# Attention rows divided by their sums inside the transposing product, with a scaled identity as its moving operand

## The reference

```python
sc = einsum(q, k) * scale          # with a causal, banded or bias mask
p = softmax(sc, axis=-1)
o = einsum(p, v)
# differential: pd = p[:, 0] - lam * p[:, 1], then o = einsum(pd, v)
```

## Time and profile before

| | |
|---|---|
| median of 3 runs | 2713.63 us (2712.52 to 2717.51) |
| profiled execution | 2710.46 us |
| its span, first to last instruction | 2709.1 us |
| mean granted TensorE clock | 0.932 of full |
| busy: PE, PEld, DVE, ACT, POOL | 90%, 67%, 66%, 45%, 17% |

### The profile page before, as it was taken

One profiled execution on the slowest core, in us unless ns is written; L12 is line 12 of the kernel. 1 busy time (PEld: TensorE's weight loads), 2 busy tenths in 40 slices (PEclk: granted clock), 3 DMA queues, 4 the chain that ended last, 5 costly groups with the idle time before them and its releaser, 6 DMA issues.

```text
span 2709.1 us, 27512 instructions
## 1 busy us (share of the span) xinstructions
PE 2437.1 (90%) x10999; PEld 1808.0 (67%) x10999; DVE 1797.2 (66%) x2013; ACT 1220.8 (45%) x1435; POOL 455.4 (17%) x467
## 2 busy tenths in 40 slices
PE   3986899897899889999897786999999999999997
PEld 2444698544498737454796645878787878787785
DVE  4666476476298534454565415888888888888886
ACT  1132453213254301222442115767676777777774
POOL 1045371034265100053232000000000000000000
PEclk9977999895799979999898897999999999999998
DMA  7631377461247705303365423999999999898994
GB/s 278 252 148 47 128 276 275 163 267 43 94 159 279 271 26 221 141 4 128 132 269 218 176 100 123 337 355 340 348 341 353 341 347 348 336 354 335 359 346 180
DMA packets 49504, 625.78 MB, mean 231 GB/s; under 512 B 8551, under 2 KB 9240, under 8 KB 11672
## 3 DMA queue, kind: packets, MB, share of 16 engines
q1 hardware_dynamic: 43632, 618.42, 60.4%
q10 hardware_dynamic: 4072, 5.40, 0.7%
q0 software_dynamic: 1664, 0.11, 0.0%
HBM read 622.85 MB, written 1.05 MB: 230 GB/s over the span
## 4 chain that ended last, share of the span: by engine, by line
PE 78%; DVE 10%; ACT 4%; issue 3%; DMA 2%; POOL 2%; ACTq 0%; DVEq 0%; SPq 0%; POOLq 0%
PE psum L1068 17%; PE psum L1069 17%; PE psum L1070 17%; PE psum L957 5%; PE psum L984 4%; DVE sbuf L684 4%; PE psum L2106 3%; PE psum L1101 2%; PE psum L1146 2%; PE psum L2100 2%; DVE ring_r L1063 1%; PE psum L2014 1%; DMA ring<-in_t_ffn 1%; PE psum L829 1%; PE psum L2588 1%
## 5 line engine op out<-in xcount | busy, mean ns | idle before, releaser
L1063 DVE TENSOR_TENSOR ring_r<-ring,sbuf_r 128x2048 fp32r<-128x2048 f32 (+1 forms) x309 | 566.6, 1837 | 183.0 <-ACT sbuf_r L1054 182.0
L1069 PE MATMUL psum<-ring_r,sc_r 128*128 128x512 f32 x1688 | 667.6, 396 | 0.0
L1054 ACT CAST sbuf_r<-ring 128x2048 fp32r<-128x2048 f32 (+1 forms) x309 | 468.6, 1518 | 359.9 <-PE psum L1070 307.9
L1063 DVE TENSOR_TENSOR ring_r<-ring,sc_r 128x2048 fp32r<-128x2048 f32 (+1 forms) x221 | 451.5, 2048 | 148.9 <-ACT sc_r L1054 147.2
L1054 ACT CAST sc_r<-ring 128x2048 fp32r<-128x2048 f32 (+1 forms) x221 | 374.3, 1700 | 264.8 <-PE psum L1070 163.5
L1068 PE MATMUL psum<-sbuf_r,sc_r 128*128 128x512 f32 (+1 forms) x1236 | 466.4, 377 | 14.7 <-DVE sc L2430 14.0
L1070 PE MATMUL psum<-sbuf_r,sc_r 128*128 128x512 f32 x948 | 375.5, 396 | 0.0
L1069 PEld LDWEIGHTS psum<-ring_r,sc_r 128*128 128x128 f32 x1688 | 318.8, 189 | 73.9 <-issue 3.1
L684 DVE SCALAR_TENSOR_TENSOR sbuf<-ring,sbuf 128x512 f32<-128x512 f32 x416 | 341.6, 824 | 21.8 <-DMA ring<-in_t_ada 16.2
L1068 PE MATMUL psum<-sc_r 128*128 128x512 f32 x740 | 299.3, 405 | 1.0 <-DVE sc_r L2620 1.0
L1070 PE MATMUL psum<-sc_r 128*128 128x512 f32 x740 | 291.1, 393 | 0.0
(11 more groups left out here) (293 smaller groups left out, 2901.4 us busy)
## 6 DMA issues: line engine op xcount, KB each, us to landing
ring<-in_t_moe SPq DMA_DIRECT2D x168, 2048.0 KB, 7.8
ring<-in_t_ada SPq DMA_DIRECT2D x48, 2048.0 KB, 8.3
ring<-in_t_mlp SPq DMA_DIRECT2D x32, 2048.0 KB, 8.5
ring<-in_t_win SPq DMA_DIRECT2D x17, 2048.0 KB, 8.3
ring<-in_t_ffn SPq DMA_DIRECT2D x16, 2048.0 KB, 8.4
ring<-in_t_out SPq DMA_DIRECT2D x7, 2048.0 KB, 8.3
ring<-in_t_bias SPq DMA_DIRECT2D x2, 2048.0 KB, 10.4
ring<-in_t_win SPq DMA_DIRECT2D x1, 1664.0 KB, 8.8
```

The source lines that it names most:

```text
L1054: p.act.e.copy(p.r(hi), src).then_inc(*p.sig("high", st.tag, n))
L1063: p.dve.e.tensor_tensor(p.r(src), src, p.r(hi), ALU.subtract).then_inc(*p.sig("lowp", st.tag, n))
L1069: e.matmul(out, l[0], r[1], start=False, stop=False)
```

## The change

Exponentials are no longer divided by their sums before they are transposed. POOL makes a diagonal matrix of 128x128 from the identity and the reciprocals of the job, and for a "second" job times the negated lambda as well. PE multiplies: the block of exponentials is the stationary operand, the diagonal the moving one, and the product is the transposed block with each query's column divided by its sum. It is an FP32 matmul in place of a transpose. For a differential pair both jobs are multiplied into the same PSUM block, the first with `start`, the second with `stop`; the mix on DVE and its small multiply are gone. The reciprocal is moved to the end of DVE's round, behind the evacuations of older jobs. Each stage has three or four buffers for diagonals (`DG`), and a diagonal waits until the product that read its buffer last is done.

```diff
@@ def pe_turned(p, A, i):
-    p.pe.wait_ge(*scaled_at(p, A, i))
+    p.pe.wait_ge(*p.at("diag", A.tag, i))
...
+    jobs = (i - 1, i) if j.kind == "second" else (i,)
     for m, c in enumerate(j.blocks):
-        ins = p.pe.e.transpose(tp[:, 128 * m:128 * m + 128], A.P[i % len(A.P)][:, c:c + 128], p.IDENT)
+        for q in jobs:
+            ins = p.pe.e.matmul(tp[:, 128 * m:128 * m + 128], A.P[q % len(A.P)][:, c:c + 128], A.DG[q % len(A.DG)],
+                                start=(q == jobs[0]), stop=(q == i))
     ins.then_inc(*p.sig("turned", A.tag, j.nth))
@@ def dve_softmax(p, A, i):   (now dve_max and dve_over)
     e.tensor_reduce(nd, sp[:, 0:j.cols], X_AXIS, ALU.max, negate=True).then_inc(*p.sig("max", A.tag, i))
+def dve_over(p, A, i):
     p.dve.wait_ge(*p.at("exp", A.tag, i))
     e.reciprocal(sm, sm).then_inc(*p.sig("over", A.tag, i))
-    if j.kind == "second":
-        pa = A.P[i % 4][:, 0:j.cols]
-        p.dve.wait_ge(*p.at("over", A.tag, i))
-        p.dve.link(e.tensor_tensor(sm, sm, p.LAM[:, 2:3], ALU.mult))
-        p.dve.wait_ge(*p.at("scaled", A.tag, i - 1))
-        e.scalar_tensor_tensor(out=pa, in0=pa, scalar=sm, in1=A.P[(i - 1) % 4][:, 0:j.cols], op0=ALU.mult,
-                               op1=ALU.add).then_inc(*p.sig("mixed", A.tag, i))
@@ def act_exp(p, A, i):
-        if A.jobs[k].kind == "first":
-            p.act.wait_ge(*p.at("mixed", A.tag, k + 1))
-        else:
-            p.act.wait_ge(*p.at("turned", A.tag, A.jobs[k].nth))
+        p.act.wait_ge(*used_at(p, A, k))
@@ def pool_scale(p, A, i):   (now pool_diag)
-    pa = A.P[i % len(A.P)][:, 0:j.cols]
     p.pool.wait_ge(*p.at("over", A.tag, i))
-    p.pool.e.tensor_scalar(pa, pa, p.SUMS[:, i % 8:i % 8 + 1], None, ALU.mult).then_inc(*p.sig("scaled", A.tag, i))
+    if i >= len(A.DG):
+        p.pool.wait_ge(*used_at(p, A, i - len(A.DG)))
+    sm, out = p.SUMS[:, i % 8:i % 8 + 1], A.DG[i % len(A.DG)]
+    if A.jobs[i].kind == "second":
+        ins = p.pool.e.tensor_scalar(out, p.IDENT, sm, p.LAM[:, 2:3], ALU.mult, ALU.mult)
+    else:
+        ins = p.pool.e.tensor_scalar(out, p.IDENT, sm, None, ALU.mult)
+    ins.then_inc(*p.sig("diag", A.tag, i))
@@ def dve_round(p, A, one, two, end):
     if one is not None:
-        dve_softmax(p, A, one)
+        dve_max(p, A, one)
     if two is not None:
         put_turned(p, p.dve, "D", A, two)
     if end is not None:
         put_values(p, p.dve, "D", A, end)
+    if one is not None:
+        dve_over(p, A, one)
```

More of the change, by code:

```diff
@@ L447, in stages @@
         self.dil = dil = Heads("dil", [U[:, i, 1440:2208] for i in range(2)], [xn[:, 0:1536], sc[:, 18432:19968]],
-                               [(0, 1), (2, 3)], [(4, 5)], 1)
+                               [(0, 1), (2, 3)], [(4, 5)], 1, [sc[:, 19968 + 128 * i:20096 + 128 * i] for i in range(3)])
         every = self.MASKB.rearrange("p (g s n) -> p g s n", g=3, s=2)[:, :, 1, :]
@@ L468, in stages @@
         self.mla = mla = Heads("mla", [sc[:, 16896 + 256 * i:17152 + 256 * i] for i in range(4)],
-                               [xn[:, 512 * i:512 * i + 512] for i in range(2)], [(i,) for i in range(4)], [(4,), (5,)], 2)
+                               [xn[:, 512 * i:512 * i + 512] for i in range(2)], [(i,) for i in range(4)], [(4,), (5,)], 2,
+                               dil.DG)
         for h in range(8):
@@ L491, in stages @@
                                [sc[:, 13312 + 512 * i:13824 + 512 * i] for i in range(2)],
-                               [(i,) for i in range(4)], [(4,), (5,)], 3)
+                               [(i,) for i in range(4)], [(4,), (5,)], 3,
+                               [sc[:, 16640 + 128 * i:16768 + 128 * i] for i in range(4)])
         for h in range(4):
@@ L539, in stages @@
         self.na = na = Heads("na", [sc[:, 6168 + 512 * i:6680 + 512 * i] for i in range(4)], [XN[:, i, :] for i in range(2)],
-                             [(i,) for i in range(3)], [(3,), (4,)], 2)
+                             [(i,) for i in range(3)], [(3,), (4,)], 2, [sc[:, 14400 + 128 * i:14528 + 128 * i] for i in range(4)])
         for h in range(16):
@@ L612, with __init__ @@
 class Heads:
-    def __init__(self, tag, P, PT, s_banks, t_banks, depth):
+    def __init__(self, tag, P, PT, s_banks, t_banks, depth, DG):
         self.tag, self.P, self.PT, self.s_banks, self.t_banks, self.depth = tag, P, PT, s_banks, t_banks, depth
+        self.DG = DG
         self.jobs, self.heads, self.groups, self.turned = [], [], 0, []
@@ L1102, in pe_scores, with used_at @@
     ins.then_inc(*p.sig("score", A.tag, i))
-def scaled_at(p, A, i):
-    return p.at("mixed" if A.jobs[i].kind == "second" else "scaled", A.tag, i)
+def used_at(p, A, i):
+    return p.at("turned", A.tag, A.jobs[i + 1 if A.jobs[i].kind == "first" else i].nth)
 def pe_turned(p, A, i):
@@ L1152, in group_bank, with dve_max @@
     return next(h.bank for h in A.heads if h.group == g)
-def dve_softmax(p, A, i):
+def dve_max(p, A, i):
     e = p.dve.e
@@ L1159, in dve_softmax @@
     sp = A.span(p, A.s_banks[i % len(A.s_banks)])
-    nd, sm = p.ND[:, i % 8:i % 8 + 1], p.SUMS[:, i % 8:i % 8 + 1]
     p.dve.wait_ge(*p.at("score", A.tag, i))
@@ L1168, in dve_softmax @@
         p.dve.wait_ge(*p.at("biased", i))
-    e.tensor_reduce(nd, sp[:, 0:j.cols], X_AXIS, ALU.max, negate=True).then_inc(*p.sig("max", A.tag, i))
+    e.tensor_reduce(p.ND[:, i % 8:i % 8 + 1], sp[:, 0:j.cols], X_AXIS, ALU.max, negate=True).then_inc(
+        *p.sig("max", A.tag, i))
+def dve_over(p, A, i):
+    sm = p.SUMS[:, i % 8:i % 8 + 1]
     p.dve.wait_ge(*p.at("exp", A.tag, i))
-    e.reciprocal(sm, sm).then_inc(*p.sig("over", A.tag, i))
-    if j.kind == "second":
-        pa = A.P[i % 4][:, 0:j.cols]
-        p.dve.wait_ge(*p.at("over", A.tag, i))
-        p.dve.link(e.tensor_tensor(sm, sm, p.LAM[:, 2:3], ALU.mult))
-        p.dve.wait_ge(*p.at("scaled", A.tag, i - 1))
-        e.scalar_tensor_tensor(out=pa, in0=pa, scalar=sm, in1=A.P[(i - 1) % 4][:, 0:j.cols], op0=ALU.mult,
-                               op1=ALU.add).then_inc(*p.sig("mixed", A.tag, i))
+    p.dve.e.reciprocal(sm, sm).then_inc(*p.sig("over", A.tag, i))
 def act_exp(p, A, i):
@@ L1636, in pool_even @@
         if one is not None:
-            pool_scale(p, p.dil, one)
+            pool_diag(p, p.dil, one)
         for m in range(3 * i, 3 * i + 3):
@@ L1649, in pool_even @@
         if one is not None:
-            pool_scale(p, p.mla, one)
+            pool_diag(p, p.mla, one)
     pool_seed(p, 14)
@@ L1969, in pool_odd @@
         if one is not None:
-            pool_scale(p, p.odd, one)
+            pool_diag(p, p.odd, one)
         if i == 19:
@@ L2336, in pool_mix @@
         if one is not None:
-            pool_scale(p, p.na, one)
+            pool_diag(p, p.na, one)
         if i % 4 == 3 and i < 32:
```

5 lines of the change are left out of this document (1 added, 4 removed).

## The result

| | before | after |
|---|---|---|
| median | 2712.09 us (20 runs, 2708.22 to 2717.51) | 2716.39 us (20 runs, 2712.02 to 2725.44) |
| span of the profiled execution | 2709.1 us | 2713.7 us |
| mean granted TensorE clock | 0.932 | 0.941 |

The ratio is 1.0017, 95% interval 1.001 to 1.0023: the kernel became 4.3 us slower. That is less than the 0.2% that the prediction set as its bound, so by that bound it belongs to "within", but with 20 runs on each side the interval shows a small loss. The forecast was +8.5 us, 2722 for the median; the measured median lies inside the stated range of 2704 to 2730, which is 26 us wide and has room for either sign.

A forecast was written before the change was run, and what follows sets the result against it. Mostly weight streaming with TensorE at full clock; of the attention stages, neighbourhood bound by TensorE, latent and differential heads by VectorE, dilated by GpSimd and TensorE in turn. 9 - 5 - 2.5 + 7 = +8.5 us, median 2722, range 2704 to 2730.

The forecast's parts named there:

- within: Whole kernel: difference under 0.2% (5.4 us), which can't be told from none; chance 0.32.
- The likeliest case: Whole kernel: odd stage's clock stays at half, neighbourhood about as costed, +8.5 us; chance 0.45.
- the halfway rival: Odd stage: clock rises in the later heads, odd +1, sum +2.5, 2716; chance 0.17.
- the last rival: Whole kernel: GpSimd waits off the path, PE's idle time takes the extra matmuls, within 3 us of 2714; chance 0.08.
- Neighbourhood, forecast +9: Neighbourhood stage: extra matmul instructions cost 0.48 us per round, partly hidden by PE idle; +9, bounds +6 and +15.4.
- Dilated, forecast -5: Dilated stage: last scaling starts some 3.5 us earlier and is 1.6 shorter, six blocks cost +1.4; -5.
- bound of -7: Dilated stage: lower bound, where the values of 4.10 us at half clock run at full.
- Latent, forecast -2.5: Latent stage: 0.3 us saved in each of eight heads, extra instructions in TensorE's idle time; -2.5, bounds 0 and -4.
- Odd, forecast +7: Odd stage at half clock: differential heads +2, later heads +5.5; together +7, bounds +4 and +10.
- a clock above 0.5 in 619 to 690: Odd stage: named as a sign that the prediction is wrong.
- the early rival: Odd stage: full clock before about the third differential head, odd -10, sum -8.5, 2705; chance 0.2.
- The full price in the neighbourhood stage: Neighbourhood stage: all extra instructions exposed, +15.4 in place of 9, odd at half clock; sum +15, 2729; chance 0.1.

The follow-up runs named there:

- e11: Kernel before with each transpose of the neighbourhood stage issued twice: median 2723.38 us in one run, neighbourhood stage 129.9 us.
- e2: Kernel before with only VectorE's new order (reciprocal behind the evacuations) in all four stages: median 2706.21 us, ratio 0.9967.
- e10: Kernel after with the reciprocal back at its old place, diagonals and products kept in all four stages: median 2722.07 us, ratio 1.0031 to the kernel before.
- e9: e4 with GpSimd writing each diagonal of the dilated stage two or three times: median 2709.94 us in one run, dilated stage 59.3 us.
- e8: Kernel after with diagonals in the dilated stage alone, scaling and transposes elsewhere, new order everywhere: median 2699.26 us, ratio 0.9952 to the kernel before.
- e7: Kernel after with each product with a diagonal in the odd stage issued twice: median 2717.68 us in one run, odd stage 91.0 us.
- e12: Same kernel as e4, run again beside e8: median 2704.6 us, ratio 0.9968 to the kernel before.
- e4: Kernel after with diagonals only in the dilated and latent stages, scaling and transposes elsewhere, new order everywhere: median 2702.81 us, ratio 0.9959 to the kernel before.
- e1: Kernel before with each transpose made a plain FP32 matmul with the unscaled identity, all four stages: median 2726.28 us in one run.

## Why the prediction was right, and by how much it was off

The sign was right in all four stages and the mechanism in three; in the latent stage one of its two reasons is not borne out. The likeliest case came about: half clock in nearly all of the odd stage, neighbourhood about as costed. The total came out 4.2 us lower than forecast (+4.3 for +8.5), 3.6 of it in the stages, because three terms were mis-sized, all towards a loss. The number alone proves little: 2716.39 is also what the halfway rival gives (2716) and lies in the "within 3 us of 2714" of the last rival. What tells the cases apart is the stages.

- **Neighbourhood, forecast +9, measured +9.1.** Groups 15.70 for 15.6, the step per round 0.51 for 0.48, none left to VectorE. The 0.04 that was taken for the group's start without a row of its own measured 0.07 (e11). Not all of it is one sum, as the new order alone gives -1.0 here (e2), and the product without it +10.2 (e10).
- **Dilated, forecast -5, measured -6.6.** The last transposes came 4.5 us earlier into the stage, inside the 3 to 5 given, and the last values 4.4: the last diagonal began 2.5 us earlier for the 3.5 forecast and was 2.0 shorter for the 1.6, and the six blocks, forecast at +1.4, cost 0.1, at full clock. What was left out of the chosen value is the last values at full clock, -1.9 (set apart by e9). The prediction had this in its bound of -7.
- **Latent, forecast -2.5, measured -3.1.** Of its two reasons, one is shown: the order gives it alone (34.2 to 32.1 in e2). The other, that GpSimd works less beside VectorE, was put at 0.1 per round and has nothing for it: product and diagonal without the order give 34.4 (e10), and taking the diagonals back costs nothing (e8). At full clock the order gives 0.22 per head (3.78 to 3.56), about the 0.19 of one copy. That is 1.8 in eight heads. The rest isn't told apart from the clock of the stage, which was 0.75 in the kernel before, 0.89 in e2 and 0.94 in the kernel after.
- **Odd, forecast +7, measured +5.5.** Each interval was right: 8.97 for 8.9, 5.29 for 5.2. The counts were not. The differential heads have three intervals between four values, and the stretches before the first and behind the last did not grow together (+0.2 and -0.2): +1.6 for +2. The average also hides that two of the three are 8.79 and the third 9.33. Of the seven intervals between later heads only five keep the full price, 657.88 to 688.01 against 666.71 to 692.55 on PE, +4.3 for +5.5. The last two have no scores beside them, and ran partly at full clock (0.83 in 691 to 694, last values 0.84 us for 1.51): from the sixth head's values to the output projection it is 694.40 - 688.01 = 6.39 us against 699.33 - 692.55 = 6.78, 0.4 less. 1.6 + 4.3 - 0.4 is the 5.5.
- **Price of an instruction.** 0.11 at full and 0.22 at half clock held. The start of a group was taken at 0.09 in the later heads; with transposes doubled a head grew by 5.07 - 4.43 = 0.64 us, which is three instructions at 0.213, with matmuls by 0.86, which leaves 0.11 for each of its two groups.
- **VectorE's part was underrated as a whole.** The forecast gave the order a copy in a wait here and there (0.7 in the neighbourhood stage, 1 in the dilated, 1.5 in the latent, none of its own in the odd one), about 3 us. e2 measured 7.3 between the medians and 5.2 in the four stages of its trace, 1.1 of that by the clock at the end of the odd stage.

**The rivals.** The clock did not rise in the odd stage early enough to matter. The prediction named a clock above 0.5 in 619 to 690 as a sign of its being wrong, and the row shows 0.52: by the letter that sign came. It is the one rise of 3.4 us at 654.5, behind the fourth differential head's values, too late for the early rival and lost in a wait before it could be the halfway one; the later heads took 5.29 us at 0.50, as forecast. e7 shows that an early rise could be had in the differential heads. There the later ones ran at half clock after a wait; whether they would have kept full clock without that wait isn't shown. The full price in the neighbourhood stage (+15.4) is refuted by 15.70 in place of 14.33 + 1.92 = 16.25 per group on average: a part did fall into idle time. That the change does little is true of the total alone, which two opposed halves of 0.3% each produce.

What stays open: whether e8 is really 5 us under e12 and why, what makes up the order's 7.3 us beyond the stages, and why the clock of a stage differs between traces of the same code (e4 and e12).

## What to carry to other kernels

A transpose that is made to do arithmetic becomes an FP32 matmul of two instructions; it pays where the engine that did the arithmetic is on the chain and TensorE has idle time (the dilated stage, GpSimd), and costs its full price where TensorE is the bound. Decide it stage by stage: the same edit was worth -6 us in one stage and +10 in another, and the kernel with the lowest median uses it in one of four. And test separately the small reorderings that come with such a change: here, moving a reciprocal behind independent copies was worth 7 us by itself, and in the kernel after it made up for about half of the loss of the rest.

## What the runs showed of the hardware that was not expected

- FP32 matmul instructions of 128x128 cost more than as many transposes of it: 1.17 against 1.06 us for four at half clock, and at full clock a round took 0.07 us more. Their weight loads on PEld are also longer, 192 ns at the median for the products of the kernel after and 143 for the transposes of the one before; that these are the cause was not tested.
- 96 instructions issued twice cost 4.8 us only, 0.05 each, as the granted clock went from 0.50 to 1.00 among the differential heads (e7, at 632.9 us). In the later heads PE was at work back to back from 657.85 on at 0.50, and did not get it in 21 us. In the kernel after it had been back to back for 38 us, from 615.9 to 654.5, when it did.
- The dilated stage's last values took half the time (2.16 us for 4.10) though no instruction of theirs was changed: the clock of the stage was 0.86 for 0.67, with the diagonals' products and shorter waits ahead of them. Which of the two raised it stays open: e9 has the products and the long waits, and full clock in all its values (0.81 over the stage); e1 has plain matmuls and the long scalings, and 0.75. The same code got 0.82 in e4 and 0.73 in e12.
